# One pass over the residual for two norms in a row, and the delta rule's next weights copied ahead of the silus

## What is computed

```python
def rms_norm(x, g):
    xf = x.astype(jnp.float32)
    y = xf * lax.rsqrt(jnp.mean(xf * xf, axis=-1, keepdims=True) + RMS_EPS)
    return (y * g.astype(jnp.float32)).astype(x.dtype)
...
    # end of the first block
        h = h + conv_ffn(rms_norm(h, norm_ffn_g[i]), ...)
    return rms_norm(h, norm_final_g)
...
    # start of the second block
    h = rms_norm_2(x, ln1_g)
    proj = h @ w_in          # q, k, v of attention, qkv and z of the delta rule, its gates a, b
...
    # delta rule: width-5 depthwise convolution over time, then silu, then q and k normed per head
    qkv = lax.conv_general_dilated(qkv_raw, conv_w[:, None, :], padding=[(2, 2)], ...)
    qkv = jax.nn.silu(qkv)
```

## Time and profile before

| | us |
|---|---|
| median of 3 runs | 2713.65 (2712.34 to 2713.84) |
| the profiled execution's own time | 2714.64 |
| its span, first to last instruction | 2712.9 |
| busy TensorE matmul / weight load | 2284.6 (84%) / 1676.2 (62%) |
| busy VectorE, ScalarE, GpSimd | 1166.7 (43%), 858.0 (32%), 163.3 (6%) |
| mean granted TensorE clock | 0.878 |

### The profile page before, as it was taken

How to read it: one execution, slowest core, us unless ns; L and a number is a source line. 1 busy time by engine, 2 the same in 40 slices (tenths; PEclk the granted TensorE clock), 3 DMA queues, 4 the chain that set the end, 5 groups by cost and what they waited for, 6 DMA issues and landing times. The chain is left out here.

```text
span 2712.9 us, 32509 instructions
## 1 busy us (share of the span) xinstructions
PE 2284.6 (84%) x13804; PEld 1676.2 (62%) x13804; DVE 1166.7 (43%) x1846; ACT 858.0 (32%) x1275; POOL 163.3 (6%) x174
## 2 busy tenths in 40 slices
PE   6898999967998776689999888875987688877885
PEld 5777888856766665468888767664975533333332
DVE  4336665356485554456663343645434311111112
ACT  4324443246563222344442244534113110100000
POOL 0000000000002110000000000000410011111110
PEclk9888999988999776789999989876858699999988
DMA  5111322222211001212222223121004399999996
GB/s 191 63 62 62 104 98 85 96 76 87 76 63 17 14 13 40 76 64 96 107 84 96 100 72 108 47 63 22 4 32 191 134 420 418 416 406 406 400 400 253
DMA packets 106597, 377.26 MB, mean 139 GB/s; under 512 B 54960, under 2 KB 55744, under 8 KB 67536
## 3 DMA queue, kind: packets, MB, share of 16 engines
q1 hardware_dynamic: 84848, 296.44, 29.5%
q10 hardware_dynamic: 9216, 67.11, 6.0%
q0 software_dynamic: 12384, 11.58, 1.5%
HBM read 375.31 MB, written 27.53 MB: 148 GB/s over the span
## 5 line engine op out<-in xcount | busy, mean ns | idle before, releaser
L590 PE MATMUL ps<-xh,wh 128*128 128x512 f32 x1384 | 557.9, 403 | 93.0 <-DVE wl L556 44.0
L591 PE MATMUL ps<-xl,wh 128*128 128x512 f32 x1384 | 552.4, 399 | 0.0
L592 PE MATMUL ps<-xh,wl 128*128 128x512 f32 x1384 | 550.7, 398 | 0.0
L556 DVE TENSOR_TENSOR wl<-raw,wh 128x2048 fp32r<-128x2048 f32 (+2 forms) x127 | 264.4, 2082 | 317.8 <-ACT wh L550 317.8
L590 PEld LDWEIGHTS ps<-xh,wh 128*128 128x128 f32 x1384 | 268.0, 194 | 170.6 <-issue 56.2
L3105 PE MATMUL ps<-egu,XT 128*64 128x512 f32 x1088 | 272.0, 657 | 84.5 <-DMA egu<-e_up 80.4
L592 PEld LDWEIGHTS ps<-xh,wl 128*128 128x128 f32 x1384 | 267.8, 193 | 57.9
L591 PEld LDWEIGHTS ps<-xl,wh 128*128 128x128 f32 x1384 | 268.6, 194 | 56.2 <-issue 0.2
L550 ACT ACTIVATE wh<-raw 128x2048 fp32r<-128x2048 f32 (+2 forms) x127 | 220.2, 1734 | 83.2 <-PE ps L875 69.2
L3105 PEld LDWEIGHTS ps<-egu,XT 128*64 128x64 f32 x1088 | 94.2, 151 | 238.9 <-issue 225.4
L3123 DVE TENSOR_TENSOR HIDT<-ps,SIL 128x256 f32<-128x256 f32 x34 | 14.4, 425 | 350.0 <-ACT SIL L3115 350.0
(11 more groups left out here) (473 smaller groups left out, 3260.8 us busy)
## 6 DMA issues: line engine op xcount, KB each, us to landing
egu<-e_gate SPq DMA_DIRECT2D x68, 1024.0 KB, 14.5
egu<-e_up SPq DMA_DIRECT2D x68, 1024.0 KB, 25.1
ed<-e_down ACTq DMA_DIRECT2D x64, 1024.0 KB, 11.1
raw<-up SPq DMA_DIRECT2D x44, 1024.0 KB, 4.8
raw<-down SPq DMA_DIRECT2D x32, 704.0 KB, 4.0
raw<-rwkv_kr SPq DMA_DIRECT2D x8, 1024.0 KB, 4.8
raw<-in_dn SPq DMA_DIRECT2D x8, 1024.0 KB, 4.9
raw<-sgu_u SPq DMA_DIRECT2D x4, 1024.0 KB, 8.3
```

The costliest lines, as they stand in the source:

```text
L556: e.tensor_tensor(K.WL[s][:, 0:n], K.RAW[r][:, 0:n], K.WH[s][:, 0:n].bitcast(F32), SUB).then_inc(*K.w_low.mark(i))
L590: e.matmul(o, h[:, q, k], x_high[:, k], start=k == 0, stop=False)
L591: e.matmul(o, h[:, q, k], x_low[:, k], start=False, stop=False)
L592: last = e.matmul(o, l[:, q, k], x_high[:, k], start=False, stop=k == KT - 1)
```

## The change

**A.** The two norms are computed from one sweep. With r the reciprocal root of `n_fin`, the ln1 norm of h * r * fing is h * (fing * ln1) * rsqrt(mean(h² (fing² + eps)) + eps²). So during the down projection of l = 1 VectorE keeps two accumulators of the same squares: `T[0]` weighted with `FW` = fing² + eps, and `T[4]` plain. TensorE makes both sums in a row, first that of ln1. ScalarE makes ln1's reciprocal root, then the eight high halves, then `n_fin`'s root, then the weights of q/k item 1. VectorE scales by `FL` = fing * ln1 straight from H, makes the low halves and the low half of item 1, and only then norms H in place. The three small tensors FW, FL and EE (eps²) are made at the start of the feed-forward part.

**B.** In the loop over the delta rule's blocks ScalarE goes by pairs: both middle taps, the next weights, then silu and square of each. VectorE makes the low half behind the taps of the odd block.

```diff
@@ -328,8 +328,9 @@
             base, ("AR", [128, 2, KT, S]), ("KB", [128, KT, S]), ("LW", [128, KT, S]), ("OMM", [128, 48]), ("PC", [128, KT, 8]))
-        self.VF, self.HID, self.SM, self.NK, self.OMK, _ = self.lay(
-            q0, ("VF", [128, KT, S]), ("HID", [128, 4, S]), ("SM", [128, S], BF16), ("NK", [128, 8]), ("OMK", [128, 8]))
+        self.VF, self.HID, x = self.lay(q0, ("VF", [128, KT, S]), ("HID", [128, 4, S]))
+        self.SM, self.NK, self.OMK, _ = self.lay(x, ("SM", [128, S], BF16), ("NK", [128, 8]), ("OMK", [128, 8]))
+        self.FW, self.FL, self.EE, _ = self.lay(x, ("FW", [128, KT]), ("FL", [128, KT]), ("EE", [128, 1]))
         self.G, self.VT, _ = self.lay(xs0, ("G", [128, KT, S]), ("VT", [128, 4, D]))
@@ -472,7 +473,7 @@
         for name, n in (("late_groups", 4), ("rwkv_o", 8), ("n_ffn1", 1), ("up1", 44), ("down1", 8),
-                        ("n_fin", 1), ("n_ln1", 1), ("in2_qk", 8), ("in2_v0", 4), ("sq_qk", 8), ("in2_v1", 4), ("in2_ab", 1), ("in2_dn", 2),
+                        ("n_ln1", 1), ("n_fin", 1), ("in2_qk", 8), ("in2_v0", 4), ("sq_qk", 8), ("in2_v1", 4), ("in2_ab", 1), ("in2_dn", 2),
                         ("ab_turned", 1), ("in2_dn2", 10), ("sq_kq", 8), ("in2_dn12", 2), ("dn_sc", 1), ("in2_dn14", 2)):
@@ -711,6 +712,92 @@
+
+def last_gains_dve(K, e):
+    fing, ln1 = (K.PRM[:, K.pc[x]:K.pc[x] + KT] for x in ("fing", "ln1"))
+    e.tensor_tensor(K.FL[:, :], fing, ln1, MUL).then_inc(*K.normed.mark("gains"))
+    e.tensor_tensor(K.FW[:, :], fing, fing, MUL).then_inc(*K.normed.mark("weights", 0))
+    e.wait_ge(*K.normed("weights", 0))
+    e.tensor_scalar(K.FW[:, :], K.FW[:, :], K.prm("eps"), None, ADD).then_inc(*K.normed.mark("weights"))
+    e.tensor_tensor(K.EE[:, :], K.prm("eps"), K.prm("eps"), MUL).then_inc(*K.normed.mark("eps"))
+
+def last_square_act(K, e, m):
+    e.wait_ge(*K.dve_out("down1", m))
+    if m > 2:
+        e.wait_ge(*K.sumsq("n_fin", m - 3))
+    e.activation(K.T[1 + m % 3], K.H[:, m], ACT.Square).then_inc(*K.square.mark("n_fin", m))
+
+def last_residual_dve(K, e, m):
+    u = K.u["down1"] + m
+    e.wait_ge(*K.gemm_sum("down1", m))
+    e.tensor_tensor(K.H[:, m], K.ps[:, u % 8], K.H[:, m], ADD).then_inc(*K.dve_out.mark("down1", m))
+    K.board.empty(u, K.dve_out("down1", m))
+    e.wait_ge(*K.square("n_fin", m))
+    x = K.T[1 + m % 3]
+    if m == 0:
+        e.wait_ge(*K.normed("weights"))
+        e.tensor_scalar(K.T[0], x, K.FW[:, 0:1], None, MUL).then_inc(*K.sumsq.mark("n_ln1", 0))
+        e.tensor_copy(K.T[4], x).then_inc(*K.sumsq.mark("n_fin", 0))
+        return
+    e.wait_ge(*K.sumsq("n_ln1", m - 1))
+    e.scalar_tensor_tensor(K.T[0], x, K.FW[:, m:m + 1], K.T[0], MUL, ADD).then_inc(*K.sumsq.mark("n_ln1", m))
+    e.wait_ge(*K.sumsq("n_fin", m - 1))
+    e.tensor_tensor(K.T[4], K.T[4], x, ADD).then_inc(*K.sumsq.mark("n_fin", m))
+
+def rows_rstd_act(K, e, stage, room, bias):
+    u = K.u[stage]
+    e.wait_ge(*K.norm_sum(stage))
+    e.activation(room, K.ps[:, u % 8], ACT.Ln, bias=bias, scale=1.0 / D).then_inc(*K.rstd.mark(stage, "ln"))
+    K.board.empty(u, K.rstd(stage, "ln"))
+    e.wait_ge(*K.rstd(stage, "ln"))
+    e.activation(room, room, ACT.Exp, scale=-0.5).then_inc(*K.rstd.mark(stage, "r"))
+
+def last_norms_pe(K, e):
+    for stage, room in (("n_ln1", K.T[0]), ("n_fin", K.T[4])):
+        u = K.u[stage]
+        for t in K.board.emptied(u - 8):
+            e.wait_ge(*t)
+        e.wait_ge(*K.sumsq(stage, KT - 1))
+        e.matmul(K.ps[:, u % 8], K.cst("ones", 128), room, start=True, stop=True).then_inc(*K.norm_sum.mark(stage))
+
+def last_norms_act(K, e):
+    e.wait_ge(*K.normed("eps"))
+    rows_rstd_act(K, e, "n_ln1", K.T[5], K.EE[:, 0:1])
+    for k in range(KT):
+        x_high_act(K, e, "in2_qk", k, K.T[1 + k % 3], K.normed("n_ln1", k), K.XH)
+    rows_rstd_act(K, e, "n_fin", K.T[4], K.prm("eps"))
+
+def last_norms_dve(K, e):
+    def scaled(k):
+        if k > 2:
+            e.wait_ge(*K.x_low("in2_qk", k - 3))
+        e.scalar_tensor_tensor(K.T[1 + k % 3], K.H[:, k], K.FL[:, k:k + 1], K.T[5], MUL, MUL).then_inc(*K.normed.mark("n_ln1", k))
+    e.wait_ge(*K.normed("gains"))
+    e.wait_ge(*K.sumsq("n_fin", KT - 1))
+    e.wait_ge(*K.rstd("n_ln1", "r"))
+    scaled(0)
+    for k in range(KT):
+        if k + 1 < KT:
+            scaled(k + 1)
+        x_low_dve(K, e, "in2_qk", k, K.T[1 + k % 3], K.XH, K.XL)
+
+def last_norm_in_place_dve(K, e):
+    e.wait_ge(*K.rstd("n_fin", "r"))
+    for k in range(KT):
+        e.scalar_tensor_tensor(K.H[:, k], K.H[:, k], K.prm("fing", k), K.T[4], MUL, MUL).then_inc(*K.normed.mark("n_fin", k))
@@ -904,13 +991,18 @@
             next_high(K, e, K.first[down] + 2 * m + part)
-        residual_act(K, e, down, norm, m)
+        if l:
+            last_square_act(K, e, m)
+        else:
+            residual_act(K, e, down, norm, m)
     K.board.point("ACT", "ffn", l)
...
     norm_dve(K, e, f"n_ffn{l}", "ffng", 8 * l, up)
+    if l:
+        last_gains_dve(K, e)
     for m in range(2 * FT):
@@ -932,7 +1024,10 @@
             next_low(K, e, K.first[down] + 2 * m + part)
-        residual_dve(K, e, down, norm, m)
+        if l:
+            last_residual_dve(K, e, m)
+        else:
+            residual_dve(K, e, down, norm, m)
     K.board.point("DVE", "ffn", l)
@@ -1934,8 +2029,7 @@
 def layer2_pe(K, e):
-    norm_pe(K, e, "n_fin")
-    norm_pe(K, e, "n_ln1")
+    last_norms_pe(K, e)
     gemm_pe(K, e, "in2_qk", "in2_qk", 8, K.XH, K.XL)
@@ -2007,10 +2101,7 @@
 def layer2_act(K, e):
-    rstd_act(K, e, "n_fin")
-    for k in range(KT):
-        square_act(K, e, "n_ln1", k, K.H[:, k], K.normed("n_fin", k))
-    norm_act(K, e, "n_ln1", "in2_qk")
+    last_norms_act(K, e)
     for m in range(8):
@@ -2037,32 +2128,38 @@
     next_high(K, e, K.first["in2_ab"])
-    for m in range(12):
-        if m % 2 == 0:
-            next_high(K, e, K.first["in2_dn"] + m // 2)
+    def features(m):
+        dst = of_kq(K, m) if m < 8 else K.DV[:, m - 8]
+        e.wait_ge(*K.conv("in2_dn", m, 3))
+        if m >= 8:
+            e.wait_ge(*K.normed("sq_qk", m - 8))
+        e.activation(dst, K.T[m % 5], ACT.Silu).then_inc(*K.act_out.mark("in2_dn", m))
+        if m < 8:
+            e.wait_ge(*K.act_out("in2_dn", m))
+            e.activation(square_room(K, "sq_kq", m), of_kq(K, m), ACT.Square).then_inc(*K.square.mark("sq_kq", m))
+    def middle_tap(m):
         u = dn_use(K, m)
         e.wait_ge(*K.gemm_sum("in2_dn", m))
-        z = K.T[m % 5]
         if m < 5:
...
             e.wait_ge(*K.act_out("in2_dn", m - 5))
-        e.activation(z, K.ps[:, u % 8], ACT.Copy, scale=K.prm("dncw", 24 + m)).then_inc(*K.act_out.mark("in2_dn", m, "tap"))
-        dst = of_kq(K, m) if m < 8 else K.DV[:, m - 8]
-        e.wait_ge(*K.conv("in2_dn", m, 3))
-        if m >= 8:
-            e.wait_ge(*K.normed("sq_qk", m - 8))
-        e.activation(dst, z, ACT.Silu).then_inc(*K.act_out.mark("in2_dn", m))
-        if m < 8:
-            e.wait_ge(*K.act_out("in2_dn", m))
-            e.activation(square_room(K, "sq_kq", m), of_kq(K, m), ACT.Square).then_inc(*K.square.mark("sq_kq", m))
-        if m == 4:
+        e.activation(K.T[m % 5], K.ps[:, u % 8], ACT.Copy, scale=K.prm("dncw", 24 + m)).then_inc(*K.act_out.mark("in2_dn", m, "tap"))
+    next_high(K, e, K.first["in2_dn"])
+    for i in range(6):
+        middle_tap(2 * i)
+        middle_tap(2 * i + 1)
+        next_high(K, e, K.first["in2_dn"] + i + 1)
+        features(2 * i)
+        features(2 * i + 1)
+        if i == 2:
             e.wait_ge(*K.dve_delta("abs"))
...
             e.activation(K.R8[:, 1], K.R8[:, 1], ACT.Exp).then_inc(*K.act_delta.mark("a"))
-    next_high(K, e, K.first["in2_dn"] + 6)
     e.wait_ge(*K.act_delta("exp"))
@@ -2099,11 +2196,10 @@
 def layer2_dve(K, e):
-    norm_in_place_dve(K, e, "n_fin", "fing", 0)
-    for k in range(KT):
-        sumsq_dve(K, e, "n_ln1", k)
-    norm_dve(K, e, "n_ln1", "ln1", 0, "in2_qk")
-    for i in range(4):
+    last_norms_dve(K, e)
+    next_low(K, e, K.first["in2_qk"])
+    last_norm_in_place_dve(K, e)
+    for i in range(1, 4):
         next_low(K, e, K.first["in2_qk"] + i)
@@ -2113,9 +2209,8 @@
     full = {k: K.sc[k][:, :, :, :] for k in K.sc}
+    next_low(K, e, K.first["in2_dn"])
     for m in range(12):
-        if m % 2 == 0:
-            next_low(K, e, K.first["in2_dn"] + m // 2)
         u = dn_use(K, m)
@@ -2126,6 +2221,8 @@
         K.board.empty(u, K.conv("in2_dn", m, 3))
+        if m % 2:
+            next_low(K, e, K.first["in2_dn"] + m // 2 + 1)
         if m < 8:
@@ -2142,7 +2239,6 @@
             e.tensor_tensor(flat(K, "SC2"), flat(K, "SC2"), flat(K, "SC1"), MAX).then_inc(*K.dve_delta.mark("abs"))
-    next_low(K, e, K.first["in2_dn"] + 6)
     e.wait_ge(*K.act_delta("ln"))
```

## The result

| | before | after |
|---|---|---|
| median of 4 runs, us | 2713.36 (2712.34 to 2713.84) | 2681.69 (2680.82 to 2683.17) |
| ratio, 95% interval | | 0.9883 [0.9871, 0.9896] |
| span of the profiled execution, us | 2712.9 | 2680.0 |
| mean granted TensorE clock | 0.878 | 0.882 |

The change takes 31.7 us off. I had forecast 2687 in 2681 to 2696: the sign and the mechanism are right, the size is 5 short. The page of the changed kernel has 8 ScalarE operations fewer and 6 VectorE operations more. TensorE does the same 13804 matmuls in 9.8 us less of busy time (2284.6 before), at a mean granted clock of 0.882 instead of 0.878. The time is not work saved: it is waiting, and items that no longer start on a lowered clock.

The account below looks back on a forecast made before the run. TensorE, which the other engines feed, was taken as the bound: its pauses lengthen the program. A's 9.4 plus B's 17.7 gave 27.1, passed through whole from 2714.64 to 2687.5; forecast 2687, range 2681 to 2696.

Parts of the forecast that it names:

- The way to the first sum, and TensorE's start: Place A: way to ln1's sum unchanged in length; TensorE starts the q/k item at 1560.3 instead of 1574.54, 14.2 gained.
- The held table load: Place A: the first table load waits for ln1's sum because this Ln has two waits; taken at 1.28.
- The final norm's root ahead of the weights: Place A: load, Ln, load, Exp add 3.9 ahead of q/k item 1's weights; new TensorE pause of 3.4.
- Item 1 "starts slow again": Place A: q/k item 1 takes 12.3 behind the new pause, before 10.9; A gains 9.4 us.
- Place B: Delta rule's input projection: all four waits between items go, and item 6 starts at 1737.1 instead of 1754.82; 17.7 us gained.
- The two slacks of 0.8: Place B: low half's margin in the second pair (four small operations) and behind the third pair (table loads); 0.8 each.
- E + 9.3: Place B: the low half of the item after next is ready 9.3 after a TensorE item's end E; needed at E + 10.9.
- Item 6 starts slow as it did before.: Place B: the delta rule's item 6 still starts on a lowered clock behind its wait, so no gain counted there.
- The wait at 1754.82: Before item 6 in place B: TensorE's wait of 3.64 ends with the Ln at 1754.00, not with the weights.
- the swallowed gain: Rival, expert stage: it ends when it did because its stream is bound elsewhere; 2713, chance 0.03.
- the slower stream: Rival, expert stage: its DMA stream runs slower, 366 GB/s or less against 390, making the kernel slower; chance 0.015.
- Table switches: Place A: final norm's pair costs 3.9 without drains, 6.6 by the skill's page; rival of costlier switches 2691, chance 0.03.

Follow-up runs that it names:

- load_ahead: Changed kernel, with ScalarE meeting the wait for eps squared at the down projection's first square instead of at the Ln; 2680.39 us.
- root_late: Changed kernel, with the final norm's Ln and Exp behind q/k item 2's high half and the in-place products behind its low half; 2677.22 us.
- shift2: Changed kernel plus one unused ScalarE copy of 1024 elements a partition ahead of ln1's Ln; single run 2688.66 us, on another chip.
- shift4: Changed kernel plus one unused ScalarE copy of 2048 elements a partition ahead of ln1's Ln; single run 2684.99 us, on another chip.
- weights_mid: Changed kernel, with ScalarE's pair in place B as tap, silu, square, tap, weights, silu, square, so taps not paired; 2683.10 us.
- weights_last: Changed kernel, with ScalarE splitting the next weights behind both silus and squares in place B, middle taps still paired; 2695.83 us.

## Why the prediction was right, point by point

The measured 2681.69 lies 0.7 inside the stated range, and 0.3 below the narrower 2682 to 2692 that got the chance of 0.805. That it lies so low is the two restarts, which I had slow and which both came at full clock; nothing in my reasoning said so.

- *The way to the first sum, and TensorE's start.* Forecast 14.2 gained, 14.07 measured (Q-D). The second sum beside the first cost nothing.
- *The held table load.* "I take 1.28": shown in the trace of the change, and by `load_ahead`, 1.38. The listing of the instruction order had told it.
- *The final norm's root ahead of the weights.* Forecast: low half ready 15.7 after TensorE's start; measured, item 1 starts with it at 1574.21 - 1558.54 = 15.67. The length of the pause was 3.4 in the forecast and is 2.67, because item 0 takes 13.0 and not 12.3. The 12.3 was a misreading: that stretch of the earlier trace rows holds 46 of the item's 48 matmuls, and in the kernel before, too, item 0 took 12.9. `root_late` shows that these four instructions are the pause.
- *Item 1 "starts slow again".* This is a step that failed. I took the restart's cost from the pause of 2.28 and the clock stayed at 1.00: 1.6 us more gain, 11.0 for A and not 9.4. (The misread 12.3 stands on both sides of that difference, for item 0 before and for item 1 after, and drops out.) `shift2` and `shift4` show that the same item can be slow by just these 1.6.
- *Place B.* 17.7 forecast, 17.69 measured, and item by item: no wait on a low half, item 6 at 9.2 behind the end of item 5 (9.1). The two slacks of 0.8 are 0.9 and 0.6: they held, the second narrowly. (The terms of E + 9.3 add up to 9.26 before the overlaps that the sentence takes off, and to 8.9 behind them; a plain pair measures 9.05.)
- *"Item 6 starts slow as it did before."* Wrong: 11.15 instead of 13.19, 2.0 more gain, in every kernel with B's full order and in `weights_mid`. Before, the stretch ahead of it held waits of 2.41 and 3.64; now it holds 0.24 and 1.84. In `weights_last`, with 0.24 and 3.64, it is slow again (12.74). That these waits decide it is not shown.
- *The wait at 1754.82.* I took the Ln for the releaser against the row's label. The label of after says the same, and item 6 starts 0.81 or 0.82 behind the start of the first Ln whatever the label: 1754.00 to 1754.82 before, 1723.38 to 1724.19 after, and 1740.87 to 1741.68 in `weights_last`, where the weights' name is back on a wait of 3.64.
- *What comes behind.* The expert stage kept its length (S to the end 658.1 before, 658.5 after) and started 33.3 earlier. Neither the swallowed gain nor the slower stream came. (That rival's 366 GB/s is a slip: 538 x 390 / (538 + 32.5) is 368. Nothing hangs on it, since the stage moves 391.)
- *Table switches.* In the trace of the change the load at 1568.10 starts 0.01 behind the Ln's end and the Exp at 1569.40 starts 0.02 behind the load's. The 2.66 a switch of the Trainium skill ("ScalarE: Activation LUTs", "What ACT_TABLE_LOAD costs") doesn't show in this kernel; its 1.28 for the load itself does.

Together: 27.1 forecast, plus 1.6 and 2.0 for the two restarts is 30.7; the last 1.0 lies within the drift of D and of S-K (269.3 to 274.4 in kernels that don't differ there).

## What to carry to other kernels

Where two engines make an operand in turn and one of them has other work in its queue, the place of that work is worth more than its length: give the queue's next operand a place behind the last thing that frees it and ahead of everything that waits for the other engine, and check the next loop turn too, since a late operand holds the next turn's start. An order listing tells where a table load or another inserted instruction stands; a second wait at an activation that switches tables cost the load's time here, and meeting it earlier was free. Cost a clock's restart as nothing or 2 us, not as one value.

## What the runs showed that I had not expected

- TensorE's clock behind a short pause: 1.98 (`weights_mid`), 2.04, 2.44 and 2.67 at full clock; 1.98 (`shift4`), 2.28, 2.53 and 3.09 with an item of 12.8 instead of 11.2. The two kernels that were profiled twice repeat their own pattern.
- Up to D, in a part identical in its instructions but for four small ones, executions differ by 6.4 us (1435.51 to 1441.88), and from K to S by 5.1. Medians of four runs hide 2 us between kernels; distances between marks, in two traces of one kernel, repeat to 0.4.
